# Attention in a hybrid layer: four of 17 blocks of the product with V from rounded parts, and three steps moved in the engines' orders

## What is computed

```
s = jnp.einsum('bqhmd,bkhmd->bhmqk', qblk, k).astype(jnp.float32) * scale
p = jax.nn.softmax(s, axis=-1)
a = p[:, :, 0] - lam * p[:, :, 1]
return jnp.einsum('bhqk,bkhe->bqhe', a.astype(v.dtype), v)
```

## Time and profile before

| | |
|---|---|
| median of 3 runs | 1667.68 us (1665.28 to 1671.02) |
| the profiled execution | 1670.53 us, span 1668.7 us |
| busy in the span | PE 1627.9 us (98%), PEld 87%, DVE 61%, ACT 53%, POOL 46% |
| granted TensorE clock | 0.996 of full speed, mean |
| costliest groups | L813 (projections, without V) 677.6 us, L931 (scores) 315.4, L1103 (output) 103.3 + 102.0, L1005 (product with V) 276.7, L997 (transposes) 171.0 |

### The profile page before, as it was taken

The page is one execution under the profiler, slowest core; times in us unless marked ns, Lnnn a source line. Parts: engine busy times, 40 slices in busy tenths (PEclk is TensorE's granted clock), DMA queues, the critical chain, the costliest instruction groups (busy, mean ns, idle before and its releaser), DMA issues.

```text
span 1668.7 us, 25628 instructions
## 1 busy us (share of the span) xinstructions
PE 1627.9 (98%) x8476; PEld 1455.4 (87%) x8476; DVE 1019.3 (61%) x1613; ACT 876.9 (53%) x1829; POOL 765.7 (46%) x807
## 2 busy tenths in 40 slices
PE   4999999999999999999989999999999999999999
PEld 2888999999999999998968888888888888889999
DVE  4553666663343344333499988888888888744442
ACT  4664666640010100100389998898998988733320
POOL 0002898960000000000089999999999999700000
PEclk8999999999999999999999999999999999999999
DMA  9662323342131231124152232114111211264441
GB/s 366 218 208 100 122 100 111 112 145 84 58 110 52 71 107 53 59 68 121 40 128 79 82 88 78 32 35 102 44 37 36 58 38 47 73 216 177 176 158 49
DMA packets 127232, 168.47 MB, mean 101 GB/s; under 512 B 10816, under 2 KB 113728, under 8 KB 126272
## 3 DMA queue, kind: packets, MB, share of 16 engines
q1 hardware_dynamic: 122032, 163.19, 30.3%
q10 hardware_dynamic: 5136, 4.46, 0.8%
HBM read 117.54 MB, written 50.07 MB: 100 GB/s over the span
## 4 chain that ended last, share of the span: by engine, by line
PE 83%; DVE 4%; DMA 4%; ACT 3%; SPq 2%; issue 2%; POOL 1%; DVEq 0%; POOLq 0%; ACTq 0%
PE ps L813 39%; PE ps L931 13%; PE ps L1005 13%; PE ps L1103 11%; PE ps L997 6%; DVE stt L1879 1%; DMA raw<-in_w_in 1%; DMA xt<-in_xtok 1%; DMA scr<-in_xtok 1%; DMA out_y<-yo 1%; DVE e L1853 1%; ACT scr L1191 1%; SPq L536 1%; PE ps L865 0%; PE ps L866 0%
## 5 line engine op out<-in xcount | busy, mean ns | idle before, releaser
L813 PE MATMUL ps<-hT,w 128*128 128x448 f32 (+1 forms) x3360 | 677.6, 361 | 0.3 <-DVE w L1522 0.3
L813 PEld LDWEIGHTS ps<-hT,w 128*128 128x128 f32 x3360 | 621.2, 188 | 48.8 <-DVE w L1522 1.1
L931 PE MATMUL ps<-kb,qb 128*128 (+2 forms) x1272 | 315.4, 377 | 8.1 <-ACT e L1402 5.2
L1879 DVE TENSOR_REDUCE stt<-ps 128x1 f32<-128x1024 f32 x252 | 273.5, 1085 | 56.2 <-PE ps L931 55.9
L1402 ACT ACTIVATE e<-ps,stt 128x1024 f32<-128x1024 f32 x252 | 255.7, 1015 | 59.8 <-DVE stt L1879 53.5
L1005 PE MATMUL ps<-at,vb 128*128 128x256 f32 x1088 | 276.7, 380 | 0.9 <-ACT atto L1346 0.5
L763 POOL TENSOR_TENSOR stt<-stt,lamc 128x2 f32<-128x2 f32 x64 | 12.5, 196 | 501.1 <-DVE stt L1896 501.1
L931 PEld LDWEIGHTS ps<-kb,qb 128*128 128x128 f32 x1272 | 213.7, 189 | 24.7 <-issue 5.9
L1005 PEld LDWEIGHTS ps<-at,vb 128*128 128x128 f32 x1088 | 198.6, 189 | 29.2 <-ACT atto L1346 3.2
L769 POOL TENSOR_TENSOR e<-e,stt 128x384 f32<-128x384 f32 x192 | 214.3, 1116 | 5.0
L1306 ACT ACTIVATE scr<-ps 128x448 f32<-128x448 f32 (+1 forms) x40 | 20.9, 532 | 307.7 <-PE ps L813 307.7
(11 more groups left out here) (162 smaller groups left out, 1758.9 us busy)
## 6 DMA issues: line engine op xcount, KB each, us to landing
raw<-in_w_in SPq DMA_DIRECT2D x32, 512.0 KB, 4.3
qb<-spill_q SPq DMA_DIRECT2D x256, 64.0 KB, 2.3
scr<-in_xT SPq DMA_DIRECT2D x8, 1024.0 KB, 6.1
raw<-in_w_gate SPq DMA_DIRECT2D x16, 512.0 KB, 4.4
spill_k<-scr SPq DMA_DIRECT2D x32, 224.0 KB, 2.2
spill_q<-scr SPq DMA_DIRECT2D x32, 224.0 KB, 2.2
mixc<-spill_cv SPq DMA_DIRECT2D x8, 896.0 KB, 7.9
xr<-in_xT SPq DMA_DIRECT2D x4, 1792.0 KB, 13.8
```

The source lines that it names most:

```text
L813: mm = pe.matmul(out, slot_of(l, j), rhs_of(r, j), start=(i == 0 and j == 0), stop=(i == 2 and j == DJ - 1))
L931: mm = pe.matmul(out[:, c0 - k0:c1 - k0], qb[:, t, ver, m], keys, start=(ver == 0), stop=(ver == 1))
L1879: dve.tensor_reduce(stt[:, b, 0, 3 * m + c:3 * m + c + 1], pair(c), AX.X, ALU.max, negate=True).then_inc(mx_done, 1)
```

## The change

It has five parts.
- **Rounded parts of blocks 12 to 15.** DVE rounds group 3 of the transposes into `ath` (the copy, with another output type) and puts the rest into `atl` (a subtraction, new). Of V, the same four tiles of a head are split by POOL in the last pass of the convolution: SP loads them (`load_parts`), POOL copies and subtracts, SP stores both parts (`store_parts`); in the attention SP loads them with the head's V. Each of the four blocks is then three `F32R` matmuls. The order of the blocks changes: even steps compute 0 to 4 and 12 to 15, odd steps 5 to 11 and 16. `atl` has one buffer, and the even step needs group 3 of the tile transposed in the step before it, so PE waits at p = 2 for DVE's subtraction.
- **Denominators.** L1888, L1892 and L1896 move from between the maximum of p = 0 and that of p = 1 to behind the maximum of p = 1, ahead of the third piece's maximum.
- **Result.** ACT copies the product out (`att_out`) ahead of the third exponential of map 1 instead of behind it.
- **Last transpose.** In even steps the single transpose of group 4 comes behind the first part of the product.
- **glast.** The last group's gates of the convolution go to another place in SBUF, since `atl` lies where they were; one element is copied for it.

```
+SB0, SB = TGROUPS[3]
+HALVES = ([0, 1, 2, 3, 12, 4, 13, 14, 15], [5, 6, 7, 8, 9, 10, 11, 16])
+CUTS = ((0, 2, 4, 6, 9), (0, 2, 4, 6, 8))
...
+            vhl = sb("vhl", [P, 2, SB, P], F32R, vctx)
...
+            vraw = sb("vraw", [P, SB, P], F32, vctx)
...
+                ath = sb("ath", [P, 2, KT, 2 * P], F32R, hctx)
...
+            atl = sb("atl", [P, SB, 2 * P], F32R, bctx)
...
+        glast = scr[:, 0:N]
...
             def load_v(head, part):
-                j0, j1 = (0, 9) if part == 0 else (9, KT - 1)
-                sp.dma_start(vb[:, j0:j1], spill["v"][head, :, j0:j1]).then_inc(s_v[part], 16)
-                if part == 1:
-                    sp.dma_start(vb[:, KT - 1], a["cache_v"][:, head * P:(head + 1) * P]).then_inc(s_v[part], 16)
+                if part == 0:
+                    sp.dma_start(vb[:, 0:5], spill["v"][head, :, 0:5]).then_inc(s_v[0], 16)
+                    for hl in range(2):
+                        sp.dma_start(f32(vhl[:, hl]), spill["vs"][hl, head]).then_inc(s_v[0], 16)
+                else:
+                    sp.dma_start(vb[:, 5:SB0], spill["v"][head, :, 5:SB0]).then_inc(s_v[1], 16)
+                    sp.dma_start(vb[:, KT - 1], a["cache_v"][:, head * P:(head + 1) * P]).then_inc(s_v[1], 16)
...
+            def load_parts(head):
+                if head == 0:
+                    sp.wait_ge(g_done, GATE_CUT[H])
+                    for i in range(2):
+                        sp.wait_ge(v_stored[i], 16 * ((TILES + 1 - i) // 2))
+                wait(sp, vs_stored, 32 * head)
+                sp.dma_start(vraw[:], spill["v"][head, :, SB0:SB0 + SB]).then_inc(vs_in, 16)
+
+            def store_parts(head):
+                sp.wait_ge(vs_lo, head + 1)
+                for hl in range(2):
+                    sp.dma_start(spill["vs"][hl, head], f32(vhl[:, hl])).then_inc(vs_stored, 16)
...
+                    if f == H - 1 and tg < H:
+                        load_parts(tg)
                     sp.wait_ge(z_used, CV0 + CV_UNITS * f + CV * tg + 1)
                     sp.dma_start(spill["ga"][f, :, c0:c0 + n], gs[:, 0:n]).then_inc(aux_stored, 16)
+                    if f == H - 1 and tg < H:
+                        store_parts(tg)
...
+            sp.wait_ge(vs_stored, 32 * H)
             load_v(0, 0)
...
+            for head in range(H):
+                pool.wait_ge(vs_in, 16 * (head + 1))
+                pool.tensor_copy(vhl[:, 0], vraw[:]).then_inc(vs_hi, 1)
+                pool.wait_ge(vs_hi, head + 1)
+                pool.tensor_tensor(vhl[:, 1], vraw[:], f32(vhl[:, 0]), ALU.subtract).then_inc(vs_lo, 1)
...
             def product(b, half, part):
-                js = (range(0, 9), range(9, KT))[half]
-                cut = (0, 2, 4, 6, 9) if half == 0 else (0, 2, 4, 6, 8)
+                js, cut = HALVES[half], CUTS[half]
+                out = ps[:, 7, b * 2 * P:(b + 1) * 2 * P]
                 for i in range(cut[part], cut[part + 1]):
-                    mm = pe.matmul(ps[:, 7, b * 2 * P:(b + 1) * 2 * P], vb[:, js[i]], at[:, b, js[i], :],
-                                   start=(half == 0 and i == 0), stop=(half == 1 and i == len(js) - 1))
+                    j, first, last = js[i], half == 0 and i == 0, half == 1 and i == len(js) - 1
+                    if SB0 <= j < SB0 + SB:
+                        pe.matmul(out, vhl[:, 0, j - SB0], ath[:, b, j], start=first, stop=False)
+                        pe.matmul(out, vhl[:, 0, j - SB0], atl[:, j - SB0], start=False, stop=False)
+                        mm = pe.matmul(out, vhl[:, 1, j - SB0], ath[:, b, j], start=False, stop=last)
+                    else:
+                        mm = pe.matmul(out, vb[:, j], at[:, b, j, :], start=first, stop=last)
...
-                    if p == 0 and tr_last:
-                        if sc or n == NT:
-                            pe.wait_ge(expc_done, 2 * n)
-                        transposes(n - 1 - S_TR, (t - 1 - S_TR) % 4, 4)
+                    if p == 0 and tr_last and not (pv and t % 2 == 0):
+                        last_block(n, t, sc)
                     if pv:
...
-                                pe.wait_ge(t_dve, n - 3)
+                        if p == 2 and half == 0:
+                            pe.wait_ge(t_dve, n - 2)
                         product(b, half, p)
+                    if p == 0 and tr_last and pv and t % 2 == 0:
+                        last_block(n, t, sc)
...
                 for p in range(4):
                     m, c = p // 2, p % 2
+                    if out and p == 3:
+                        att_out(it, t)
                     if sc and p == 3:
                         wait(act, a1_ready, n - 1)
                         exp_third(n, t, 1)
-                    if out and p == 3:
-                        att_out(it, t)
...
                 if t % 2 == 0:
-                    wait(dve, pv_mm, n - 2)
-                dve.tensor_copy(at[:, t // 2, j0:j0 + cnt, (t % 2) * P:(t % 2 + 1) * P],
-                                trbank(3).rearrange("p (j q) -> p j q", j=cnt)).then_inc(t_dve, 1)
+                    wait(dve, pv_mm, n - 1)
+                cols = slice((t % 2) * P, (t % 2 + 1) * P)
+                src = trbank(3).rearrange("p (j q) -> p j q", j=cnt)
+                dve.tensor_copy(ath[:, t // 2, j0:j0 + cnt, cols], src).then_inc(t_dvh, 1)
+                dve.wait_ge(t_dvh, n + 1)
+                dve.tensor_tensor(atl[:, :, cols], src, f32(ath[:, t // 2, j0:j0 + cnt, cols]), ALU.subtract).then_inc(t_dve, 1)
...
-                    if sc and p == 1:
-                        max_third(n, t, 0)
-
-                    if p == 0 and tr_last:
-                        tr_dve(n - 1 - S_TR, (t - 1 - S_TR) % 4)
-                    if p == 0 and den:
+                    if p == (1 if sc else 0) and den:
                         dve.wait_ge(f_done, n)
                         dve.tensor_tensor(stt[:, 1 - b, 4, :], stt[:, 1 - b, 3, :], stt[:, 1 - b, 1, :], ALU.mult)\
                             .then_inc(fz_done, 1)
...
+                    if sc and p == 1:
+                        max_third(n, t, 0)
+
+                    if p == 0 and tr_last:
+                        tr_dve(n - 1 - S_TR, (t - 1 - S_TR) % 4)
```

## The result

The changed kernel takes 1682.38 us, median of 4 runs (1679.75 to 1684.88), beside 1668.08 for the kernel before (median of 4, 1665.28 to 1671.02): ratio 1.0087, 95% interval 1.0074 to 1.0099. It is slower by 14 us; the prediction said 1669.3 and reached to 1677. The place and the sign that it named for its second rival (VectorE and ACT's chain, slower) are what happened, and more so.

The account below looks back on a forecast made before the run. The prediction took GpSimd's loop (9.05 + 0.50 us a step) as the bound, TensorE just below. Terms 0.5 + 1.5 - 0.6 + 0.2 = +1.6 on the median 1667.68 gave 1669.3 us, range 1657 to 1677.

Parts of the forecast that it names:

- second rival: Steady attention steps: VectorE and ACT's chain is the bound, deciding from 9.60 us on; with 9.69, total 1677 us; chance 0.19.
- The bound before: Attention steps: GpSimd's 9.05 us of work plus 0.50 us waiting for VectorE's reciprocal make 9.55; TensorE is 0.05 us below.
- The product: Blocks 12 to 15 on TensorE: 0.36 us each instead of 0.43, saving 0.29 us every second step.
- TensorE's pace of 9.35: TensorE's own attention step after the change, 9.35 us instead of 9.50; counts only if TensorE is the bound.
- The subtraction: New VectorE instruction for the rest of the rounded transposes: 0.69 us (0.62 to 0.80), without lengthening the GpSimd loop.
- The denominators' move: Moving VectorE's three denominator instructions takes no work or latency out of GpSimd's loop; the step stays 9.55 us.
- the term for VectorE's arrival: VectorE's chain within a steady step, counted from the reciprocal: reaches L1888 at 9.18, next reciprocal at 9.56 us if free.
- the steady part of +0.5 us: The 48 attention steps from 990 us on: step stays 9.55 (9.54 to 9.70), costing +0.5 us (0 to +7).
- The combine's late start: VectorE's L1853 probably comes 0.04 us too late, waits for GpSimd's fourth scaling to begin, ends at 4.29 instead of 3.70.
- The first steps: First 16 attention steps, 0.69 us more on VectorE each: +1.5 us (-2 to +4).
- Up to the first combine: Before the attention's first combine: one tiny copy added for `glast`, +0.2 us; V's splitting falls on idle GpSimd.
- The tail: After 1452 us the time is TensorE's: two products, -0.6 us.

Follow-up runs that it names:

- the cut add: Kernel before, with GpSimd's second addition of the biases (1600 to 2176) cut into two at 2016: 1662.63 us, ratio 0.997.
- the last two kernels above: Changed kernel, first scaling cut at 1488, second addition in two, VectorE's loop written out; plus w_out preparation behind the combine 1672.51 us, or early denominators in old place 1664.28 us.
- the moves alone: Kernel before with the denominators' and the result's new places and the last transpose behind the product, no rounding: 1669.97 us, ratio 1.002.
- 464 columns: Changed kernel with GpSimd's first two scalings 464 columns wide instead of 384 and the next two 304: 1675.92 us, ratio 1.0059.
- the two omissions: Preparation of w_out's rest left out, rounded part read twice: in the changed kernel 1676.88 us, ratio 1.0072; in the kernel before 1660.72 us, ratio 0.9966.
- 416 columns: Changed kernel with GpSimd's first two scalings 416 columns wide instead of 384 and the next two 352: 1686.59 us, ratio 1.0133.

## Why the prediction was wrong

**The bound before: right.** The loop of GpSimd's 9.05 us and VectorE's three small instructions was real: the cut add opens it, and the steps then go by TensorE's blocks.

**The product: right.** A block of three fp32r matmuls was put at 0.36 us, 0.119 each. The changed kernel's TensorE timeline:

```profile
1228.24 0.28 PE L1052 MATMUL ps<-ath,vhl 128*128 128x256 f32 x1
...
1229.18 0.28 PE L1054 MATMUL ps<-ath,vhl 128*128 128x256 f32 x1
```

Nine matmuls in a row, 0.94 us for eight spacings: 0.118 each, 0.35 a block (0.119 and 0.36 in the prediction; by the 0.109 that it quotes beside it, its own sum would be 9.30 rather than the 9.31 it gives). TensorE's pace of 9.35 is the mean step of the last two kernels above.

**The subtraction: right in size** (0.69 us), and right that it doesn't lock GpSimd: with it gone, GpSimd's wait is that of before again and nothing else of its work is shorter.

**The denominators' move: right for the loop**, as the moves alone show.

**The step that failed is the term for VectorE's arrival**: "9.18, and if free 0.19 + 0.19 to the next reciprocal: 9.56", and with it the steady part of +0.5 us. The sum gives rows for the other hand-overs, but none for one of them: from L1764 to the maximum "0.10". In the trace of before the two are 0.10 apart only in the first steps, which are written out; in its loop the wait for TensorE hides what they need. With VectorE's loop written out the changed kernel has 0.11 there, and the rest of the chain is as forecast: counted from the reciprocal, the combine ends at 4.29 (4.29 in the prediction), L1824 starts at 5.72 (5.73) and L1950 at 9.15 (9.18). Then the step is 9.55 and the 48 steps cost +0.9 us beside before, near the +0.5 of the prediction. In the loop it is 0.21, and 0.50 at each turn. That is most of the difference: 464.8 - 458.0 = 6.8 of the 7.7 us. The prediction saw that two bounds lay 0.01 us apart (9.55 and 9.56), and gave the forecast 0.61 all the same; where an unlocked chain and a locked loop are that close, every 0.1 us that the trace hides behind a wait decides, and here the trace of before hid it behind VectorE's 0.22 us for TensorE. The second rival was therefore worth more than 0.19. Its price, put at 7 us of steps, came out at 7.7, but partly by luck: it stood for a subtraction of 0.8 us or slower hand-overs between engines, and what came was VectorE's own loop control. The combine's late start was in the sum (4.29 us instead of 3.70), so it is no fault of the forecast, though taking it away (464 columns) or taking the subtraction away also gives the loss back.

**The first steps: +1.5 predicted, +4.4 measured.** The prediction names the w_out parts among what makes these steps long, but it prices the subtraction alone and doesn't look at the new neighbours of what it moved. The preparation of w_out's rest now follows the reciprocal and holds GpSimd's small product. By the two omissions 2.5 us of it are that; the moves alone account for 3.4 us. The two can't be added, since they overlap, and what of the last 1.9 us is subtraction and what is chain stays open. What the 0.9 us are that the old place of the denominators gives back stays open too.

**The rest.** Up to the first combine +1.6 instead of +0.2: the first combine starts between 840.1 and 843.5 us over all kernels here, whatever was changed behind it, so this is within what executions differ by. The tail: -3.2 instead of -0.6, but not as a gain of the change; the lower clock's stretch in the tail of the profiled kernel before (below) is missing in that of the changed one. Among the tails without such a stretch, the two in the order of before take 218.2 and 218.3 us and that of the changed kernel 219.5 (219.6 with 416 columns), so the tail got 1.2 us longer, not 0.6 shorter. One pause that the prediction's term for the tail lacks is this one of the changed kernel, in its last steps, for the subtraction; in the kernel before TensorE has none over 0.6 us between 1440 and 1490 us:

```profile
1458.45 0.66 PE L1042 MATMUL ps<-cst,e 128*128 128x128 f32 x4 [2.27 <-DVE atl L1914]
```

The medians differ by 14.3 us, 3.85 more than the profiled executions, because the profiled one of before lay 2.45 above its median and that of the changed kernel 1.40 below. A tail of +1.2 in place of -3.2 would give 14.9 for the two traces, but since only the profiled executions have a tail that can be read, that the other executions differ in this way stays an inference.

## What to carry to other kernels

When two loops lie within 0.1 us of each other, write the second one out instruction by instruction with its register and branch instructions, since an engine's loop control is free only as long as that engine waits once in the step: written out, it gave back 6.8 us of the steady steps here. Before moving an instruction, list what runs beside its new place on the other engine; a six-number product can cost 1.3 us next to the wrong neighbour, and moving the neighbour in turn can cost more. And shorten the instruction that another engine must wait out before moving the waiting one: one cut add made the kernel before 0.3% faster.

## What the runs showed of the hardware that was not expected

**Who gets the shared port.** A combine whose record began 0.04 us ahead of GpSimd's scaling still waited for it to end; one 0.20 us ahead went first. The start in a record isn't the moment that decides; somewhere between these two leads it does. The Trainium skill ("SBUF — State Buffer", Who interferes with whom) gives the lock for a whole instruction, which the 1.67 and 1.81 us records bear out.

**Loop control of VectorE.** 0.10 us in a step with waits on register values, 0.29 more at a turn with compare-and-branch, both invisible in busy time and only partly in the waits (as "issue").

**The clock in the tail.** TensorE runs at the lower of its two clocks (1.2 of 2.4 GHz) for some 3 us at a time in eleven of the 17 traced tails, and the table sorts by it: the six tails without such a stretch take 218.2 to 219.6 us, the six with one 221.3 to 223.8, and the five with two 223.4 to 224.0. In the kernel with VectorE's loop written out, the first stretch comes behind a pause of 2.3 us as the attention ends (TensorE's timeline, then a window):

```profile
1452.24 1.12 PE L1042 MATMUL ps<-cst,e 128*128 128x128 f32 x4 [2.32 <-DVE atl L1914]
```

```profile
1452.00:1455.00 3.00, 2.76 (x11) 2.48 (x12) 1.72 (x2) 1.78 (x3) 2.88 (x4) 0.51 1.04 388
```

A second such stretch follows near 1507 us (granted 0.61 from 1506 to 1509). The kernel before has one, near 1496, behind a pause of 1.9 us:

```profile
1496.06 0.47 PE L1082 MATMUL ps<-csh,onesr 128*128 128x448 f32 x1 [1.88 <-DVE csl L1919]
```

```profile
1496.00:1499.40 3.40, 3.34 (x11) 3.02 (x12) 3.33 (x7) 2.63 (x5) 0.00 (x0) 0.65 0.18 67
```

The changed kernel has both pauses as well, 2.27 us at 1458.45 (above) and one of 1.69 us at 1510.36, and no stretch at the lower clock from 1440 us to the end:

```profile
1440.00:1679.00 239.00, 230.41 (x1190) 212.34 (x1189) 116.43 (x197) 80.18 (x157) 26.10 (x28) 1.00 0.42 148
```

So some 2 to 5 us of such a comparison may be decided behind the changed part, by whether the clock falls after a pause, and a pause of the same length on the same line was followed by it in one trace and not in the other. Each kernel's tail was seen in one execution only; whether the kernel or the execution decides stays open.
